# Shifted places for the halves of each weight piece, and wide and narrow matmuls in turn in every second FFN piece

## The chip, the cores and the metric

The kernel runs on one core of one Trainium2 chip. What counts is the device time of one execution, in microseconds (us). TensorE is called PE here (its weight loads PEld), VectorE is DVE, ScalarE is ACT, GpSimd is POOL and SyncE is SP.

## What is computed

Two blocks run one after the other on 256 rows of width 1024 in float32. Each has two layers, and each layer is an FFN, a mixer (attention and scan branches with gates) and a second FFN. Cut to the part that the change touches, one FFN is:

```
def swiglu(h, w_gate, w_up, w_down):
    a = h @ w_gate            # 256x1024 @ 1024x2816
    u = h @ w_up
    return (silu(a) * u) @ w_down      # 256x2816 @ 2816x1024

for l in range(2):                     # first block; the second has the same shape with layer norms
    x = x + 0.5 * swiglu(rms_norm(x), ...)
    x = x + hybrid_mixer(rms_norm(x), ...)     # input projection, three branches, gates, output projection
    x = x + 0.5 * swiglu(rms_norm(x), ...)
```

There are eight such FFNs in all. Every weight is used once, so some 500 MB of weights stream through the core.

## The kernel before, in words

**Precision in three products.** Weights and activations are float32. The kernel splits each into a high half of type float32r and a low half, the rest. A product is three matmuls: high activation with high weight, low activation with high weight, high activation with low weight.

**Pieces.** `plan()` cuts all weights into 938 pieces, numbered i, most of them 128 partitions by 1024 columns. SP loads blocks of up to two pieces into one of three `raw` buffers. ACT copies a piece into its high half (`whi`, L1777), and DVE, for a few pieces POOL, subtracts to get the low half (`wlo`, L2038 and L2498). There are five buffers of each half (`NHL = 5`), and piece i uses buffer i % 5 of both. Its halves are overwritten by those of piece i + 5, once PE has signalled the end of piece i (`mm`).

**Where buffers lie.** `LINE = 256`: the transposed activations (`xT_both`, `hT1`, `hT2`, `cq` and others) start at the same place within 256 bytes as the buffers `whi` and `wlo`. In the kernel before, raw, whi, wlo, xT_both and hT all start 128 bytes past a multiple of 256, and each of a piece's halves starts at the first byte of its buffer.

**PE's three ways to use a piece.** `rows` (L1544) loads a 128x128 block of the activations as the stationary operand and streams up to 512 columns of the weight piece. `columns` (L1563) loads 128 columns of the weight piece and streams 256 columns of activations. `wide` (L1579, L1585) does the FFN's gate and up projections: with 128 columns of `whi` loaded, one matmul streams 512 columns, the high and the low half of the activations together (called wide below); with 128 columns of `wlo` loaded, one streams 256, the high half alone (called narrow below). A piece holds four k-tiles of 256 columns, so `wide` issues eight wide matmuls into two PSUM banks and then eight narrow ones into the second halves of the same banks. Each of the eight FFNs has 20 chunks of two such pieces (320 pieces, 2560 wide and 2560 narrow matmuls); its first chunk and its down-projection use `rows`.

**What sets the order.** `Order` records one list of steps in program order, and each engine runs its own kinds of step from it. Halves are made up to four pieces ahead of the piece that PE works on. Every engine waits on semaphores; within `wide` PE waits for the high half at the start of a piece and for the low half ahead of the narrow matmuls.

Of the kernel before, what the change touches and what calls it, by code (L numbers as in the profile page):

```python
# [10 lines left out]
F32R = mybir.dt.float32r  # L11
# [8 lines left out]
PIECE = 1024  # L20
# [149 lines left out]
class Signals:  # L170
# [14 lines left out]
    def at(self, kind, *key):  # L185
        return self.sems[kind], self.value[(kind, key)] if self.sure else 0
# [54 lines left out]
        self.xt, self.H, self.L, self.nk, self.outs, self.free = xt, xt.H, xt.L, nk, outs, free  # L241


def memory(nc, ctx):

    m = {}

    def sbuf(name, shape, dt=F32, scope=ctx):
        m[name] = scope.enter_context(nc.sbuf_tensor(name, shape, dt))
        return m[name]  # L250

    def lined(name, scope=ctx):

        rest = (at_line - nc.sbuf_base) % LINE // 32 * 32
        if rest:
            scope.enter_context(nc.sbuf_tensor(name + "_rest", [128, rest // 4], F32))

    def halves(name, nk, scope=ctx):
        lined(name, scope)
        m[name] = Halves(name, sbuf(name + "_hi", [128, nk, 256], F32R, scope),  # L260
                         sbuf(name + "_lo", [128, nk, 256], F32R, scope), nk)

    def many(name, n, shape, dt=F32, scope=ctx):
        m[name] = [sbuf(f"{name}{i}", shape, dt, scope) for i in range(n)]

    m["ps"] = [ctx.enter_context(nc.psum_tensor(f"ps{i}", [128, 512], F32)) for i in range(8)]
    many("raw", NRAW, [128, BLOCK])
    many("whi", NHL, [128, PIECE], F32R)
    at_line = nc.sbuf_base % LINE
    many("wlo", NHL, [128, PIECE], F32R)  # L270
    many("x", 2, [128, D])
    sbuf("xn", [128, 2, D])
    sbuf("ident", [128, 128])
    sbuf("cols", [128, NCOLS])
    sbuf("stat", [128, 512])
    sbuf("phalf", [128, 2])
    lined("xT")
    both = sbuf("xT_both", [128, 2, 8, 256], F32R)
    m["xT"] = Halves("xT", both[:, 0, :, :], both[:, 1, :, :], 8, both)

    def ffn(block):
        with ExitStack() as ph:
            halves("hT" + block, 22, ph)
            many("h" + block, 3, [128, 2, 256], F32, ph)
            sbuf("row" + block, [128, 256], F32, ph)

    with ExitStack() as b1:
        sbuf("rope1", [128, 2, 64], F32, b1)
        sbuf("causal", [128, 384], F32, b1)
        sbuf("dist", [128, 4, 384], F32, b1)  # L290
        ffn("1")
        with ExitStack() as ph:
            sbuf("qk1", [128, 18, 256], F32, ph)
            sbuf("v1", [128, 2, 1152], F32, ph)
            sbuf("o_dil3", [128, 2, 768], F32, ph)
            sbuf("o_dil", [128, 2, 256], F32, ph)
            halves("oTa", 3, ph)
            halves("oTb", 3, ph)
            many("sm1_", 2, [128, 384], F32, ph)
            many("pr1_", 3, [128, 384], F32, ph)  # L300
            many("pt1_", 2, [128, 384], F32, ph)
            with ExitStack() as pm:
                sbuf("lat", [128, 2, 416], F32, pm)
                sbuf("q_mla", [128, 2, 576], F32, pm)
                sbuf("k_mla", [128, 2, 576], F32, pm)
                sbuf("v_mla", [128, 2, 384], F32, pm)
                halves("cq", 2, pm)
                halves("ckv", 1, pm)
                sbuf("rope_a", [128, 2, 96], F32, pm)
                sbuf("rope_b", [128, 2, 96], F32, pm)  # L310
                many("qkT", 2, [96, 512], F32, pm)
            sbuf("g1", [128, 2, 3072], F32, ph)
    many("vr", 2, [128, D])
    sbuf("strict", [128, 384])
    sbuf("chunk", [128, 384])
    sbuf("rope2", [128, 2, 32])
    sbuf("ends", [128, 384])
    ffn("2")
    with ExitStack() as ph:
        sbuf("oa", [128, 2, 1024], F32, ph)  # L320
        sbuf("ob", [128, 2, 1024], F32, ph)
        many("sm2_", 2, [128, 385], F32, ph)
        many("pr2_", 3, [128, 384], F32, ph)
        many("pt2_", 2, [128, 384], F32, ph)
        sbuf("rw", [128, 272], F32, ph)
        sbuf("g2", [128, 6144], F32, ph)
        with ExitStack() as reg2:
            sbuf("bc", [128, 4, 256], F32, reg2)
            sbuf("xd", [128, 2, 1024], F32, reg2)
            many("sums", 2, [128, 4, 256], F32, reg2)  # L330
            many("decay", 2, [128, 4, 384], F32, reg2)
            sbuf("cb", [128, 2, 384], F32, reg2)
            many("conv", 3, [128, 256], F32, reg2)
            many("rot", 2, [128, 512], F32, reg2)
            many("rot_t", 2, [128, 128], F32, reg2)
            sbuf("dt8", [128, 8, 16], F32, reg2)
        sbuf("qkc", [128, 16, 256], F32, ph)
        sbuf("vc", [128, 2, 1024], F32, ph)
        halves("oT2", 8, ph)
    return m  # L340


class Order:
# [53 lines left out]
    def halve(self, part):  # L397
        i = self.split[part]
        b, off, n = self.where[i]
        raw = self.m["raw"][b % NRAW][:, off:off + n]  # L400
        hi, lo = self.m["whi"][i % NHL][:, 0:n], self.m["wlo"][i % NHL][:, 0:n]
        if part == 0:
            self.do("hi", i, b, hi, raw)
        else:
            self.lo_of[i] = ("lo_p" if i in self.on_pool else "lo", i)
            self.do(self.lo_of[i][0], i, lo, raw, hi, self.hold)
        self.split[part] += 1
        self.ahead()
# [1118 lines left out]
def tensor_program(engine, sg, m, steps, *_):  # L1527
# [2 lines left out]

    def rows(i, t, job, lo_there, ready, banks):
        _, w, kts = pieces[i]
        hi, lo = m["whi"][i % NHL], m["wlo"][i % NHL]
        pe.wait_ge(*at("hi", i))
        for f in job.free[t]:
            pe.wait_ge(*at(*f))
        sl = slice(128 * t, 128 * t + 128)
        for n, (xs, ws) in enumerate(((job.H, hi), (job.L, hi), (job.H, lo))):
            if n == 2:
                pe.wait_ge(*at(*lo_there))  # L1540
            for j, (_, kt, _) in enumerate(kts):
                pe.wait_ge(*at(*ready[j]))
                for bank, c0, c1 in [job.outs[t][b] for b in banks if b < len(job.outs[t])]:
                    made = e.matmul(bank[:, 0:c1 - c0], xs[:, kt, sl], ws[:, j * w + c0:j * w + c1],  # L1544
                                    start=kt == 0 and n == 0, stop=kt == job.nk - 1 and n == 2)
        made.then_inc(*mark("mm", i, t, *(banks if banks == (0,) else ())))

    def columns(i, job, lo_there, ready):
        _, w, kts = pieces[i]
        hi, lo = m["whi"][i % NHL], m["wlo"][i % NHL]  # L1550
        pe.wait_ge(*at("hi", i))
        for freed in job.free:
            for f in freed:
                pe.wait_ge(*at(*f))
        for n, (ws, xs) in enumerate(((hi, job.H), (hi, job.L), (lo, job.H))):
            if n == 2:
                pe.wait_ge(*at(*lo_there))
            for j, (_, kt, _) in enumerate(kts):
                for there in ready[j]:
                    pe.wait_ge(*at(*there))  # L1560
                for c, out in enumerate(job.outs):
                    o = j * w + 128 * c
                    made = e.matmul(out, ws[:, o:o + 128], xs[:, kt, :], start=kt == 0 and n == 0 and c % 2 == 0,  # L1563
                                    stop=kt == job.nk - 1 and n == 2, skip_group_check=True)
        made.then_inc(*mark("mm", i, 1))

    def wide(i, job, lo_there, ready):
        _, w, kts = pieces[i]
        hi, lo = m["whi"][i % NHL], m["wlo"][i % NHL]
        pe.wait_ge(*at("hi", i))  # L1570
        for freed in job.free:
            for f in freed:
                pe.wait_ge(*at(*f))
        for j, (_, kt, _) in enumerate(kts):
            for there in ready[j]:
                pe.wait_ge(*at(*there))
            for c, bank in enumerate(job.outs):
                o = j * w + 128 * c
                e.matmul(bank[:, :].rearrange("p (n x) -> p n x", n=2), hi[:, o:o + 128], job.xt.both[:, :, kt, :],  # L1579
                         start=kt == 0, stop=False, skip_group_check=True)  # L1580
        pe.wait_ge(*at(*lo_there))
        for j, (_, kt, _) in enumerate(kts):
            for c, bank in enumerate(job.outs):
                o = j * w + 128 * c
                made = e.matmul(bank[:, 256:512], lo[:, o:o + 128], job.H[:, kt, :], start=False,  # L1585
                                stop=kt == job.nk - 1, skip_group_check=True)
        made.then_inc(*mark("mm", i, 1))

    def dt_rows(i, job, lo_there, ready):
        _, w, kts = pieces[i]  # L1590
        hi, lo = m["whi"][i % NHL], m["wlo"][i % NHL]
        pe.wait_ge(*at("hi", i))
        pe.wait_ge(*at(*lo_there))
        for f in job.free[0]:
# [1030 lines left out]
```

## Time and profile before

| what | value |
|---|---|
| device time, median of 2 runs | 2814.43 us (2814.07 to 2814.79) |
| span of the profiled execution | 2812.3 us |
| PE busy | 2792.6 us, 99% of the span, 15556 matmuls |
| PEld busy | 2396.6 us, 85% |
| DVE busy | 1921.3 us, 68% |
| ACT busy | 1554.0 us, 55% |
| POOL busy | 241.5 us, 9% |
| DMA | 503.82 MB, 50.2% of 16 engines' time on the weight queue |
| mean granted clock of PE | 0.999 |

The table tells what share of the span an engine was at work. The profile of one execution has its own time in its span alone, from the first to the last instruction; the device time of the runs lies 2.1 us above it. PE's matmuls overlap each other, so a busy share says little of how fast they follow one another: that is read from the starts in the timeline.

### The profile page before, as it was taken

Reading aid. Unit: us, or ns where it says so; the run is one execution under the profiler, and the core shown is the slowest. Engines: PE = TensorE matmul, PEld = TensorE weight load, DVE = VectorE, ACT = ScalarE, POOL = GpSimd, SP = SyncE. Lnnn points to the kernel's source line nnn. Section 1 sums busy time; section 2 is a strip of 40 time slices with the busy share of each in tenths; the row PEclk is TensorE's granted clock in tenths of the full one; section 3 lists DMA queues with packets and bytes.
Section 4 is the critical chain, followed back from the end, with each engine's and each line's share of the span. In section 5 each row is a group of like instructions: output and inputs, shape, how many; then the busy total and the mean of one; then the engine's idle time right before and its main releaser. Section 6 shows DMA issues by size and latency. Waiting matters only on the chain.

```text
span 2812.3 us, 40293 instructions
## 1 busy us (share of the span) xinstructions
PE 2792.6 (99%) x15556; PEld 2396.6 (85%) x15556; DVE 1921.3 (68%) x3180; ACT 1554.0 (55%) x2718; POOL 241.5 (9%) x187
## 2 busy tenths in 40 slices
PE   9999999999999999999999999999999999999998
PEld 8889888888889888888888987888888888878887
DVE  6756676747655667756568777776566687777765
ACT  6545656545545656545456556455455465655553
POOL 0010011010010011010014100110100141001100
PEclk9999999999999999999999999999999999999999
DMA  6544445555544345555554344555555554445553
GB/s 242 191 171 158 149 156 182 193 185 190 195 167 152 139 172 194 199 190 195 195 193 179 136 163 159 210 194 182 199 189 195 183 187 153 158 156 184 209 185 135
DMA packets 75055, 503.82 MB, mean 179 GB/s; under 512 B 8784, under 2 KB 10480, under 8 KB 19184
## 3 DMA queue, kind: packets, MB, share of 16 engines
q1 hardware_dynamic: 74576, 501.07, 50.2%
q8 instruction: 124, 2.03, 0.3%
q14 instruction: 67, 0.55, 0.1%
q10 hardware_dynamic: 288, 0.17, 0.0%
HBM read 500.12 MB, written 1.08 MB: 178 GB/s over the span
## 4 chain that ended last, share of the span: by engine, by line
PE 93%; DVE 4%; POOL 2%; issue 1%; ACT 1%; DMA 0%; SPq 0%; DVEq 0%; ACTq 0%
PE ps L1544 45%; PE ps L1579 21%; PE ps L1585 11%; PE ps L1563 9%; PE ps L1606 3%; POOL wlo L2498 2%; DVE wlo L2038 1%; PE ps L1701 1%; PE ps L1699 1%; DVE conv L2327 1%; PE ps L1726 1%; PE ps L1716 0%; PE ps L1717 0%; PE ps L1718 0%; DVE ps L2144 0%
## 5 line engine op out<-in xcount | busy, mean ns | idle before, releaser
L1777 ACT ACTIVATE whi<-raw 128x1024 fp32r<-128x1024 f32 (+3 forms) x938 | 977.5, 1045 | 600.3 <-PE ps L1544 426.1
L2038 DVE TENSOR_TENSOR wlo<-raw,whi 128x1024 fp32r<-128x1024 f32 (+2 forms) x894 | 1084.1, 1220 | 219.9 <-ACT whi L1777 218.9
L1579 PE MATMUL ps<-xT_both,whi 128*128 128x512 f32 x2560 | 641.6, 393 | 0.0
L1544 PE MATMUL ps<-whi,xT_both 128*128 128x512 f32 (+2 forms) x2336 | 628.9, 391 | 2.6 <-DVE xT_both L2061 1.6
L1579 PEld LDWEIGHTS ps<-xT_both,whi 128*128 128x128 f32 x2560 | 461.1, 189 | 82.6
L1544 PEld LDWEIGHTS ps<-whi,xT_both 128*128 128x128 f32 x2336 | 425.5, 188 | 83.7 <-issue 9.3
L1585 PEld LDWEIGHTS ps<-xT_both,wlo 128*128 128x128 f32 x2560 | 349.3, 191 | 24.9
L1585 PE MATMUL ps<-xT_both,wlo 128*128 128x256 f32 x2560 | 357.1, 282 | 0.0
L1544 PE MATMUL ps<-wlo,xT_both 128*128 128x512 f32 (+2 forms) x1168 | 354.6, 385 | 0.3 <-DVE wlo L2038 0.3
L2118 DVE TENSOR_TENSOR h<-h,ps 128x256 f32<-128x256 f32 x320 | 127.0, 418 | 203.1 <-ACT h L1826 203.1
L1544 PEld LDWEIGHTS ps<-wlo,xT_both 128*128 128x128 f32 x1168 | 218.4, 188 | 43.7 <-DVE wlo L2038 1.4
L1826 ACT ACTIVATE h<-ps 128x256 f32<-128x256 f32 x320 | 105.4, 382 | 214.1 <-PE ps L1585 214.1
L1544 PE MATMUL ps<-whi,hT_hi 128*128 128x512 f32 x704 | 221.5, 390 | 0.0
L1544 PE MATMUL ps<-whi,hT_lo 128*128 128x512 f32 x704 | 220.9, 389 | 0.0
L1544 PE MATMUL ps<-wlo,hT_hi 128*128 128x512 f32 x704 | 220.8, 389 | 0.0
L2498 POOL TENSOR_TENSOR wlo<-raw,whi 128x1024 fp32r<-128x1024 f32 (+1 forms) x44 | 102.5, 2347 | 1293.7 <-ACT whi L1777 1291.7
L1563 PE MATMUL ps<-xT_both,whi 128*128 128x256 f32 x1472 | 196.1, 286 | 1.0 <-DVE v_mla L2254 1.0
L1563 PEld LDWEIGHTS ps<-xT_both,whi 128*128 128x128 f32 x1472 | 182.9, 191 | 7.7 <-issue 6.9
L1544 PEld LDWEIGHTS ps<-wlo,hT_hi 128*128 128x128 f32 x704 | 132.2, 188 | 27.5
L1544 PEld LDWEIGHTS ps<-whi,hT_lo 128*128 128x128 f32 x704 | 132.2, 188 | 27.3
L1544 PEld LDWEIGHTS ps<-whi,hT_hi 128*128 128x128 f32 x704 | 131.7, 188 | 26.5
L1563 PE MATMUL ps<-xT_both,wlo 128*128 128x256 f32 x736 | 103.2, 283 | 0.0
(315 smaller groups left out, 2526.7 us busy)
## 6 DMA issues: line engine op xcount, KB each, us to landing
raw<-in_w SPq DMA_DIRECT2D x435, 1024.0 KB, 4.8
vr<-in_vrows SPq DMA_DIRECT2D x19, 512.0 KB, 5.6
raw<-in_w SPq DMA_DIRECT2D x12, 768.0 KB, 4.3
raw<-in_w SPq DMA_DIRECT2D x10, 896.0 KB, 4.5
sums<-scratch SPq DMA_DIRECT2D x8, 512.0 KB, 4.4
raw<-in_w SPq DMA_DIRECT2D x4, 832.0 KB, 4.4
raw<-in_w SPq DMA_DIRECT2D x4, 576.0 KB, 3.7
raw<-in_w SPq DMA_DIRECT2D x4, 512.0 KB, 6.9
```

Of the source, the lines that this page charges most:

```text
L1544: made = e.matmul(bank[:, 0:c1 - c0], xs[:, kt, sl], ws[:, j * w + c0:j * w + c1], start=kt == 0 and n == 0, stop=kt == job.nk - 1 and n == 2)
L1563: made = e.matmul(out, ws[:, o:o + 128], xs[:, kt, :], start=kt == 0 and n == 0 and c % 2 == 0, stop=kt == job.nk - 1 and n == 2, skip_gro ...
L1579: e.matmul(bank[:, :].rearrange("p (n x) -> p n x", n=2), hi[:, o:o + 128], job.xt.both[:, :, kt, :], start=kt == 0, stop=False, skip_grou ...
L1585: made = e.matmul(bank[:, 256:512], lo[:, o:o + 128], job.H[:, kt, :], start=False, stop=kt == job.nk - 1, skip_group_check=True)
L1606: return e.transpose(out, in_, ident[0:k, 0:k])
L1699: e.matmul(ps[:, 0:128], qT[:, 0:128], kT[:, 0:128], start=True, stop=True)
L1701: e.matmul(ps[:, 128:384], qT[:, 128:256], kT[:, 0:256], start=True, stop=True).then_inc(*mark("att", "s", *key))
L1777: e.activation(out, raw, ACT.Copy).then_inc(*mark("hi", i))
L1826: e.activation(h[:, n, :], banks[n][:, 256:512], ACT.Copy).then_inc(*mark("copy_a", "part", s, c, n))
L2038: e.tensor_tensor(out, raw, hi.bitcast(F32), sub).then_inc(*mark("lo", i))
L2118: e.tensor_tensor(h[:, n, :], h[:, n, :], banks[n][:, 0:256], add).then_inc(*mark("summed", s, c, n))
L2498: e.tensor_tensor(out, raw, hi.bitcast(F32), ALU.subtract).then_inc(*mark("lo_p", i))
```

## The change

Two things are changed. First, the halves of piece i no longer start at the first byte of their buffers: `upper` and `lower` add an offset of 0 to 240 bytes in steps of 16, another for each half and piece, and the buffers are 256 bytes longer for it. The place of everything else within 256 bytes stays as it was (all still start at 128). To make room, the scratch area for dynamic DMAs at the start of SBUF is set to 8192 bytes per partition, from 16384. Second, in `wide`, pieces with an odd number issue each narrow matmul right behind the wide one of the same k-tile and bank, and wait for both halves at the start of the piece. Even pieces stay as they were.

```diff
+SLACK = 64
+
+
+def upper(m, i):
+    at = 4 * ((7 * i + i // 16) % 16)
+    return m["whi"][i % NHL][:, at:at + PIECE]
+
+
+def lower(m, i):
+    at = 4 * ((3 * i + 5 * (i // 32)) % 16)
+    return m["wlo"][i % NHL][:, at:at + PIECE]
...
-    many("whi", NHL, [128, PIECE], F32R)
+    many("whi", NHL, [128, PIECE + SLACK], F32R)
     at_line = nc.sbuf_base % LINE
-    many("wlo", NHL, [128, PIECE], F32R)
+    many("wlo", NHL, [128, PIECE + SLACK], F32R)
...
-        hi, lo = self.m["whi"][i % NHL][:, 0:n], self.m["wlo"][i % NHL][:, 0:n]
+        hi, lo = upper(self.m, i)[:, 0:n], lower(self.m, i)[:, 0:n]
...
     def wide(i, job, lo_there, ready):
         _, w, kts = pieces[i]
-        hi, lo = m["whi"][i % NHL], m["wlo"][i % NHL]
+        hi, lo = upper(m, i), lower(m, i)
         pe.wait_ge(*at("hi", i))
         for freed in job.free:
             for f in freed:
                 pe.wait_ge(*at(*f))
+        woven = i % 2 == 1
+        if woven:
+            pe.wait_ge(*at(*lo_there))
         for j, (_, kt, _) in enumerate(kts):
             for there in ready[j]:
                 pe.wait_ge(*at(*there))
...
                 e.matmul(bank[:, :].rearrange("p (n x) -> p n x", n=2), hi[:, o:o + 128], job.xt.both[:, :, kt, :],
                          start=kt == 0, stop=False, skip_group_check=True)
-        pe.wait_ge(*at(*lo_there))
-        for j, (_, kt, _) in enumerate(kts):
-            for c, bank in enumerate(job.outs):
-                o = j * w + 128 * c
-                made = e.matmul(bank[:, 256:512], lo[:, o:o + 128], job.H[:, kt, :], start=False,
-                                stop=kt == job.nk - 1, skip_group_check=True)
+                if woven:
+                    made = e.matmul(bank[:, 256:512], lo[:, o:o + 128], job.H[:, kt, :], start=False,
+                                    stop=kt == job.nk - 1, skip_group_check=True)
+        if not woven:
+            pe.wait_ge(*at(*lo_there))
+            for j, (_, kt, _) in enumerate(kts):
+                for c, bank in enumerate(job.outs):
+                    o = j * w + 128 * c
+                    made = e.matmul(bank[:, 256:512], lo[:, o:o + 128], job.H[:, kt, :], start=False,
+                                    stop=kt == job.nk - 1, skip_group_check=True)
         made.then_inc(*mark("mm", i, 1))
...
-    nc = _bacc.Bacc("TRN2", target_bir_lowering=False, num_devices=1)
+    nc = _bacc.Bacc("TRN2", target_bir_lowering=False, num_devices=1, dynamic_dma_scratch_size=8192)
```

`rows`, `columns` and `dt_rows` take `hi, lo = upper(m, i), lower(m, i)` in the same way.

This is PE's order in the first FFN before, behind the first chunk of two pieces: two pieces (an even and an odd one), each with its wide matmuls (L1579) and then its narrow ones (L1585).

```order
L1579 MATMUL ps<-xT_both,whi 128x512 [waits s_hi]
L1579 MATMUL ps<-xT_both,whi 128x512 x7
L1585 MATMUL ps<-xT_both,wlo 128x256 [waits s_lo]
L1585 MATMUL ps<-xT_both,wlo 128x256 x7
L1579 MATMUL ps<-xT_both,whi 128x512 [waits s_hi]
L1579 MATMUL ps<-xT_both,whi 128x512 x7
L1585 MATMUL ps<-xT_both,wlo 128x256 [waits s_lo]
L1585 MATMUL ps<-xT_both,wlo 128x256 x7
```

The same two pieces now (wide matmuls are L1595, narrow ones L1605 in an even piece and L1598 in an odd one); the odd piece's last pairs are left out.

```order
L1595 MATMUL ps<-xT_both,whi 128x512 [waits s_hi]
L1595 MATMUL ps<-xT_both,whi 128x512 x7
L1605 MATMUL ps<-xT_both,wlo 128x256 [waits s_lo]
L1605 MATMUL ps<-xT_both,wlo 128x256 x7
L1595 MATMUL ps<-xT_both,whi 128x512 [waits s_lo,s_hi]
L1598 MATMUL ps<-xT_both,wlo 128x256
L1595 MATMUL ps<-xT_both,whi 128x512
L1598 MATMUL ps<-xT_both,wlo 128x256
L1595 MATMUL ps<-xT_both,whi 128x512
L1598 MATMUL ps<-xT_both,wlo 128x256
```

In the odd piece the wait for the low half moved from behind eight wide matmuls to the start of the piece, and the narrow matmuls moved up between the wide ones. The end of the first FFN's last chunk, where PE goes on to the down-projection, now reads:

```order
L1595 MATMUL ps<-xT_both,whi 128x512
L1598 MATMUL ps<-xT_both,wlo 128x256
L1595 MATMUL ps<-xT_both,whi 128x512
L1598 MATMUL ps<-xT_both,wlo 128x256
L1557 MATMUL ps<-whi,hT_hi 128x512 [waits s_summed,s_xlo,s_hi]
```

A narrow matmul is still the last of the chunk, so what waits for the chunk's end waits for the same instruction. The other engines issue the same instructions in the same order.

## Rows read from the trace of the kernel before

**Rows 1.** the page: span, busy share of each engine, granted clock in slices.

```profile
span 2812.3 us, 40293 instructions
...
PE 2792.6 (99%) x15556; PEld 2396.6 (85%) x15556; DVE 1921.3 (68%) x3180; ACT 1554.0 (55%) x2718; POOL 241.5 (9%) x187
...
PEclk9999999999999999999999999999999999999999
```

**Rows 2.** the page's chain that ended last, shares of the span by line.

```profile
PE ps L1544 45%; PE ps L1579 21%; PE ps L1585 11%; PE ps L1563 9%; PE ps L1606 3%; POOL wlo L2498 2%; DVE wlo L2038 1%; PE ps L1701 1%; PE ps L1699 1%; DVE conv L2327 1%; PE ps L1726 1%; PE ps L1716 0%; PE ps L1717 0%; PE ps L1718 0%; DVE ps L2144 0%
```

**Rows 3.** groups by line and shape: count | busy us, mean ns | idle before.

```profile
L1579 PE MATMUL ps<-xT_both,whi 128*128 128x512 f32 x2560 | 641.6, 393 | 0.0
L1544 PE MATMUL ps<-whi,xT_both 128*128 128x512 f32 x2080 | 571.7, 397 | 1.0 <-ACT whi L1777 0.8
...
L1585 PE MATMUL ps<-xT_both,wlo 128*128 128x256 f32 x2560 | 357.1, 282 | 0.0
...
L1544 PE MATMUL ps<-wlo,xT_both 128*128 128x512 f32 x1040 | 321.5, 390 | 0.3 <-DVE wlo L2038 0.3
L1544 PE MATMUL ps<-whi,hT_hi 128*128 128x512 f32 x704 | 221.5, 390 | 0.0
...
L1563 PE MATMUL ps<-xT_both,whi 128*128 128x256 f32 x1472 | 196.1, 286 | 1.0 <-DVE v_mla L2254 1.0
```

**Rows 4.** timeline of PE in FFN pieces: start us, length us, operation, count.

```profile
64.19 2.00 PE L1579 MATMUL ps<-xT_both,whi 128*128 128x512 f32 x8
66.03 1.12 PE L1585 MATMUL ps<-xT_both,wlo 128*128 128x256 f32 x8
66.99 2.00 PE L1579 MATMUL ps<-xT_both,whi 128*128 128x512 f32 x8
...
69.78 2.00 PE L1579 MATMUL ps<-xT_both,whi 128*128 128x512 f32 x8
```

**Rows 5.** timeline of PE, the last two wide matmuls of one piece.

```profile
65.58 0.61 PE L1579 MATMUL ps<-xT_both,whi 128*128 128x512 f32 x2
```

**Rows 6.** timeline of PE in the down-projection, 512 columns throughout.

```profile
141.76 0.61 PE L1544 MATMUL ps<-wlo,hT_hi 128*128 128x512 f32 x2
...
144.48 0.61 PE L1544 MATMUL ps<-wlo,hT_hi 128*128 128x512 f32 x2
```

**Rows 7.** timeline of PE at the pieces of 256 columns, L1563.

```profile
1469.85 2.08 PE L1563 MATMUL ps<-xT_both,whi 128*128 128x256 f32 x16
...
1481.37 0.59 PE L1737 MATMUL ps<-bc 128*128 128x256 f32 x2
1481.80 0.39 PE L1738 MATMUL ps<-bc 128*128 128x128 f32 x2
```

**Rows 8.** timeline of PE at the piece with 16-column weight loads.

```profile
1451.88 0.39 PE L1600 MATMUL ps<-xT_both,whi 128*16 128x256 f32 x2
...
1454.69 2.07 PE L1563 MATMUL ps<-xT_both,whi 128*128 128x256 f32 x16
```

**Rows 9.** timeline of PE at the pieces of 288 columns.

```profile
218.13 0.43 PE L1544 MATMUL ps<-whi,cq_hi 128*128 128x288 f32 x2
...
221.06 0.43 PE L1544 MATMUL ps<-wlo,cq_hi 128*128 128x288 f32 x2
```

**Rows 10.** groups of DVE by line and shape.

```profile
L2038 DVE TENSOR_TENSOR wlo<-raw,whi 128x1024 fp32r<-128x1024 f32 x852 | 1051.8, 1240 | 218.7 <-ACT whi L1777 217.7
...
L2122 DVE TENSOR_TENSOR h<-h,row 128x256 f32<-128x256 f32 x80 | 34.1, 426 | 2.7
...
L2438 DVE TENSOR_TENSOR pr<-pr,sm 128x384 f32<-128x384 f32 x32 | 17.9, 559 | 1.1
```

**Rows 11.** timeline of ACT over the same FFN pieces.

```profile
69.98 1.07 ACT L1777 ACTIVATE whi<-raw 128x1024 fp32r<-128x1024 f32 x1 [0.88 <-PE ps L1585]
```

**Rows 12.** timeline of DVE over the same pieces, two of its halvings.

```profile
64.62 1.22 DVE L2038 TENSOR_TENSOR wlo<-raw,whi 128x1024 fp32r<-128x1024 f32 x1
...
70.20 1.22 DVE L2038 TENSOR_TENSOR wlo<-raw,whi 128x1024 fp32r<-128x1024 f32 x1
```

More of the change, by code:

```diff
@@ L1549, in columns @@
         _, w, kts = pieces[i]
-        hi, lo = m["whi"][i % NHL], m["wlo"][i % NHL]
+        hi, lo = upper(m, i), lower(m, i)
         pe.wait_ge(*at("hi", i))
@@ L1568, in wide @@
         _, w, kts = pieces[i]
-        hi, lo = m["whi"][i % NHL], m["wlo"][i % NHL]
+        hi, lo = upper(m, i), lower(m, i)
         pe.wait_ge(*at("hi", i))
@@ L1590, in dt_rows @@
         _, w, kts = pieces[i]
-        hi, lo = m["whi"][i % NHL], m["wlo"][i % NHL]
+        hi, lo = upper(m, i), lower(m, i)
         pe.wait_ge(*at("hi", i))
```

## The prediction, made before the changed kernel ran

> **What bounds the kernel now.** I read the page first: PE is busy for 2792.6 of 2812.3 us at full granted clock in every slice [rows 1], and the chain that ended last runs through PE's piece lines, L1544, L1579, L1585 and L1563, for 86% of the span [rows 2]. Then the groups by line: the matmuls that use weight pieces waited about 1 us for anything, those of the FFN nothing at all [rows 3]. So the time is the number of matmuls by the distance from one start to the next, and only a change of that distance moves it. A busy mean (393 ns for a wide matmul) is not that distance, since matmuls overlap. I take it from starts in the timeline:
>
> - 512 columns in the down-projection: from 141.76 to 144.48 us lie 12 matmuls, 226.7 ns each [rows 6]. 512 columns at 2.4 GHz are 213.3 ns, so each carries 13.3 ns more.
> - 256 columns: from 1469.85 to 1481.37 us four pieces of 24, 96 matmuls, 120.0 ns each [rows 7]. Columns are 106.7, and again 13.3 more.
> - An even and an odd FFN piece: 64.19 to 69.78 us is 5.59, so 2.795 us a piece [rows 4]. At 226.7 and 120.0 its sixteen matmuls would take 8 x 346.7 = 2.773 us. The odd 20 ns are in the wide ones: the first six take 64.19 to 65.58, 231.7 ns each, the last two 0.45 us, 225 to 227 each [rows 4, 5]. After the step from narrow to wide PE needs some matmuls to come to its steady distance. The narrow ones take (66.99 - 66.03) / 8 = 120.
>
> **The change part by part.**
>
> *Alternation.* It adds and removes no matmul: 160 of the 320 pieces, so 1280 pairs, are issued in another order. A pair costs 2.795 / 8 = 349.4 ns now. If each matmul keeps its steady distance whatever stands ahead of it, a pair costs 346.7 and the change brings 1280 x 2.7 ns = 3.5 us. The trace before has no wide matmul behind a single narrow one. Lower end: that, and the even pieces too lose their slow first six (30 ns x 160 = 4.8 us) because they no longer follow eight narrow ones: -8.3 us. Upper end: every wide matmul in a pair pays the 231.7 of a first one, 351.7 a pair: +2.9 us. I take -4 us, near the steady sum, since the step from wide to narrow shows nothing of the kind, and give the even pieces little, because an odd piece's end is still a narrow matmul.
>
> The narrow matmul now adds into the same 256 PSUM columns as the wide one just ahead. A row bears on that: the piece of 16-column loads puts three matmuls of 256 columns in a row into the same columns, and its 24 take 1451.88 to 1454.69, 117.1 ns each [rows 8], no more than 120. So no term for it. Nor does a shorter time between weight loads bind: eight narrow ones in a row already load 128 columns every 120 ns.
>
> The wait for the low half comes 1.84 us earlier in odd pieces. The cover: the piece ends at 69.78; ACT takes its buffer at 69.98 [rows 11]; DVE makes low halves in pairs 5.58 us apart (64.62 and 70.20, [rows 12]), so the one for the freed buffer stands at the latest near 74.3 (a third one, 4.1 us behind 70.20, as the first of the next pair) and ends by 75.5. PE comes to that piece four pieces later, at 69.78 + 4 x 2.795 = 80.96. Some 5 us are left where 1.84 are lost: no stall, 0 us. If that cover were gone, a woven piece would stand for up to 1.2 us (one halving); the place to see it is the first chunk of an FFN. The end of an odd piece is its last narrow matmul as before, so ACT and the buffers behind it are released at the same point; the raw buffers, and with them SP's loads, depend on ACT and DVE, whose order is unchanged.
>
> *Places.* Every one of the matmuls on pieces reads one operand (the stationary one in the FFN and in `columns`, the streamed one in `rows`) at another place within 256 bytes than now, nearly always another than that of its partner. The rows of [rows 3] are 2560 + 2560 of the FFN, 2080 + 1040 + 3 x 704 of `rows` (the 704 appear for each of the three products) and 1472 plus half as many with the low half: 12,560 matmuls; with the smaller groups some 13,300, of which some 8,200 have 512 columns. The trace has places other than 128 for three of such operands. In the pieces of 288 columns the second k-tile starts 1152 bytes on, so at 0 instead of 128; 22 matmuls take 218.13 to 221.06, 133.2 ns each, which is 120 of columns and the same 13.2 [rows 9]. The 16-column loads move by 64 bytes each and keep 117 [rows 8]. On DVE, L2438 reads an operand 4 bytes off: 559 ns for 384 columns, where 256 at an even place take 426 and 1024 take 1240 [rows 10], by which line 384 would be 562. None shows a cost, but no row has PE at a multiple of 16 that is not one of 64. I take 0, from the nearest rows. Upper bound: PE stays at the distance of its slow starts wherever it has 512 columns: 5.0 ns x 8,200 = +41 us. Lower bound: all go at the 117.1 of [rows 8] against 120: -2.9 ns x 13,300 = -39 us.
>
> The Trainium skill, "SBUF — State Buffer", section on who interferes with whom, gives PE two independent read ports, one for the streamed operand and one for the weight load. By it the relative place of the two can't matter, and the sum stays where the rows put it.
>
> ACT and DVE write the shifted halves. DVE sits idle for 218.7 us ahead of its halving, waiting for ACT [rows 10], so a few ns more on 938 of them stay covered. The smaller DMA scratch only moves addresses.
>
> *Sum.* The profiled execution's span is 2812.3 us; -4 + 0 gives 2808.3. The device time's median, 2814.43, lies 2.1 above the span; adding that gives **2810 us**.
>
> **Rivals.**
>
> *A, slower: shifted weights keep PE off its steady distance.* Mechanism: PE's steady distance depends on both operands of a matmul lying alike within 256 bytes, as all of them do now; at another place each matmul of 512 columns pays the 5 ns of a slow start. For it: those 5 ns exist and are of that size whatever buffer is read [rows 4, 5]. Against: the two places of [rows 9]. Time: 2810 + 41 = 2851. It decides from 0.3 ns a matmul on, where it eats the 4 us. A heavier form, in which a shifted weight load doubles the 13.3 ns, gives 13,300 x 13.3 = +177 us, 2987; past 2% it needs 4.5 ns on all. Chance 0.17 for the first, 0.06 for forms past 2%.
>
> *B, faster: the 13.3 ns are a collision that the new places dissolve.* For it: a float32 matmul of 256 columns (L1737) takes (1481.80 - 1481.37) / 2 = 215 ns, twice 106.7 and only 1.6 more, with weight loads of the same 128 columns [rows 7]; so the 13.3 are not due to every matmul. Against: 256, 288 and 512 columns carry the same 13.3, which looks like a fixed step and not like a collision that depends on where two streams meet. In full it gives 11.7 ns x 13,300 = -156 us, 2654; in part (117.1 for 120) 2810 - 39 = 2771. Chance 0.10 for the part, 0.05 for more than 2%. The Trainium skill, "TensorE: Matmul & The Clock Gate", section on the back-to-back issue gap, gives N/2.4 + 2.5 ns, which is 215.8 for 512 columns; this trace disagrees by 10.9 ns, and by that rule this rival is the one that restores the gap.
>
> *C, alternation costs: every wide one pays for the narrow one ahead of it.* 2814.4 + 2.9 = 2817, with places at nothing. Chance 0.12, a part of the 0.62 below.
>
> *D, the change does nothing:* 2814. It shares the forecast's range.
>
> **How the numbers follow.** Forecast with places at nothing (D and C with it): 0.62, between 2803 and 2820, likeliest 2810. A to 2851: 0.17, A past 2%: 0.06. B in part: 0.10, B past 2%: 0.05. About 2%, 56 us, is what a measurement of this kernel can tell from no change. Faster by over that: 0.05; slower: 0.06; within: 0.89. The range takes in the partial forms of A and B, **2775 to 2851**, and leaves out the far forms and a slice of the partial ones.
>
> **What would show it.** Odd pieces: the distance between the starts of two narrow matmuls in a woven piece near 346.7 ns; even pieces at 2.77 to 2.80 us; no idle ahead of L1595 and L1598. Down-projection still 226.7 ns and `columns` 120.0, whatever i is. DVE's halving still near 1240 ns, ACT's near 1.07 us. It would be wrong if distances differed from piece to piece with a period of 16, or if the down-projection, which alternation does not touch, moved.

## The result, and the profile after

The changed kernel takes 2836.83 us (median of 2 runs, 2836.57 to 2837.09) where the kernel before takes 2814.43: 1.008 times as long, 95% interval [1.0051, 1.0109]. It is slower by 22 us. The forecast was 2810 us, faster by 4.

The page of the changed kernel, its span, busy engines and chain by line, to be held against [rows 1, 2]:

```profile
span 2835.3 us, 40453 instructions
...
PE 2816.9 (99%) x15556; PEld 2390.6 (84%) x15556; DVE 1921.7 (68%) x3180; ACT 1554.7 (55%) x2718; POOL 239.3 (8%) x187
...
PE ps L1557 46%; PE ps L1595 21%; PE ps L1576 8%; PE ps L1605 5%; PE ps L1598 5%; PE ps L1626 3%; POOL wlo L2518 2%; DVE conv L2347 1%; DVE wlo L2058 1%; PE ps L1721 1%; PE ps L1719 1%; PE ps L1746 1%; ACT whi L1797 0%; ACT conv L1969 0%; PE ps L1736 0%
```

PE is still at work 99% of the span, and the chain still runs through the piece lines (L1557 is L1544 of before, L1576 is L1563, L1595 is L1579, L1605 and L1598 are L1585). The span is 23.0 us longer, PE's busy time 24.3, with the same 15556 matmuls. PE doesn't wait more: its groups by line (count, then busy us and mean ns, then idle us before) have the same idle time as in [rows 3]. DVE's halving costs what it did in [rows 10], and waits 12 us longer in all for ACT, off PE's path.

```profile
L2058 DVE TENSOR_TENSOR wlo<-raw,whi 128x1024 fp32r<-128x1024 f32 x852 | 1051.3, 1239 | 230.3 <-ACT whi L1797 229.0
...
L1595 PE MATMUL ps<-xT_both,whi 128*128 128x512 f32 x2560 | 771.2, 394 | 0.0
L1557 PE MATMUL ps<-whi,xT_both 128*128 128x512 f32 x2080 | 578.8, 400 | 1.1 <-ACT whi L1797 0.9
...
L1557 PE MATMUL ps<-whi,hT_hi 128*128 128x512 f32 x704 | 224.9, 395 | 0.0
```

So the distances have grown. The down-projection, which alternation doesn't touch, in the timeline of PE (start us, length us, operation, count):

```profile
141.83 0.62 PE L1557 MATMUL ps<-whi,hT_hi 128*128 128x512 f32 x2
...
144.61 0.62 PE L1557 MATMUL ps<-whi,hT_hi 128*128 128x512 f32 x2
```

Twelve matmuls take 2.78 us here, 231.7 ns each, where [rows 6] have 226.7. Its single distances were 226 or 227 ns in 95 of 100 cases before, and are so in 6 of 100 now: nearly all lie anywhere from 224 to 241. An FFN stretch, to be held against [rows 4]: an odd piece, an even one and the start of the next.

```profile
64.88 0.39 PE L1595 MATMUL ps<-xT_both,whi 128*128 128x512 f32 x1
65.11 0.28 PE L1598 MATMUL ps<-xT_both,wlo 128*128 128x256 f32 x1
65.23 0.39 PE L1595 MATMUL ps<-xT_both,whi 128*128 128x512 f32 x1
...
67.66 2.01 PE L1595 MATMUL ps<-xT_both,whi 128*128 128x512 f32 x8
69.51 1.11 PE L1605 MATMUL ps<-xT_both,wlo 128*128 128x256 f32 x8
70.46 0.40 PE L1595 MATMUL ps<-xT_both,whi 128*128 128x512 f32 x1
```

The woven piece takes 64.88 to 67.66, 2.78 us, the even one 67.66 to 70.46, 2.80. Neither is far from the 2.795 of before. Summed over all matmuls on pieces, from each start to the next start on PE:

| matmuls | before, us (mean ns) | changed, us (mean ns) | difference, us |
|---|---|---|---|
| down-projection, 512 columns, x2110 | 479.3 (227.1) | 490.5 (232.5) | +11.2 |
| other row pieces, 512 columns, x3648 | 855.7 (234.6) | 869.0 (238.2) | +13.3 |
| FFN, wide, x2560 | 589.5 (230.3) | 594.4 (232.2) | +4.9 |
| FFN, narrow, x2560 | 304.8 (119.1) | 301.4 (117.7) | -3.4 |
| columns, 256 columns, x2208 | 270.2 (122.4) | 267.2 (121.0) | -3.0 |
| row pieces of 288, x48 | 6.7 (139.2) | 6.7 (139.2) | 0 |

The first column has the group, its columns per matmul and how many distances were summed. The whole loss stands in the pieces that PE streams (`rows`), at 512 columns. Where PE loads the piece and streams activations, the sum is -1.5 us.

### The profile page after: what moved, and what is told of

The parts are those of the page before. It is cut to its first block, busy times and chain, and to the rows that moved or that the text cites. A ratio compares the mean times of both kernels' runs of the same rounds, so it can differ in the third digit from the quotient of the medians.

```text
span 2835.3 us, 40453 instructions
## 1 busy us (share of the span) xinstructions
PE 2816.9 (99%) x15556; PEld 2390.6 (84%) x15556; DVE 1921.7 (68%) x3180; ACT 1554.7 (55%) x2718; POOL 239.3 (8%) x187
## 4 chain that ended last, share of the span: by engine, by line
PE 93%; DVE 4%; POOL 2%; ACT 1%; issue 0%; DMA 0%; SPq 0%; DVEq 0%; ACTq 0%
PE ps L1557 46%; PE ps L1595 21%; PE ps L1576 8%; PE ps L1605 5%; PE ps L1598 5%; PE ps L1626 3%; POOL wlo L2518 2%; DVE conv L2347 1%; DVE wlo L2058 1%; PE ps L1721 1%; PE ps L1719 1%; PE ps L1746 1%; ACT whi L1797 0%; ACT conv L1969 0%; PE ps L1736 0%
## 5 line engine op out<-in xcount | busy, mean ns | idle before, releaser
L2058 DVE TENSOR_TENSOR wlo<-raw,whi 128x1024 fp32r<-128x1024 f32 (+2 forms) x894 | 1083.7, 1219 | 231.5 <-ACT whi L1797 230.3
L1595 PE MATMUL ps<-xT_both,whi 128*128 128x512 f32 x2560 | 771.2, 394 | 0.0
L1557 PE MATMUL ps<-whi,xT_both 128*128 128x512 f32 (+2 forms) x2336 | 636.3, 394 | 2.7 <-DVE xT_both L2081 1.6
L1595 PEld LDWEIGHTS ps<-xT_both,whi 128*128 128x128 f32 x2560 | 470.1, 188 | 98.3
L1557 PEld LDWEIGHTS ps<-whi,xT_both 128*128 128x128 f32 x2336 | 425.8, 188 | 90.4 <-issue 9.3
L1557 PE MATMUL ps<-wlo,xT_both 128*128 128x512 f32 (+2 forms) x1168 | 359.0, 388 | 0.3 <-DVE wlo L2058 0.3
L1598 PE MATMUL ps<-xT_both,wlo 128*128 128x256 f32 x1280 | 358.1, 280 | 0.0
L1557 PEld LDWEIGHTS ps<-wlo,xT_both 128*128 128x128 f32 x1168 | 218.7, 188 | 47.3 <-DVE wlo L2058 1.2
L1598 PEld LDWEIGHTS ps<-xT_both,wlo 128*128 128x128 f32 x1280 | 240.9, 188 | 0.1
L1557 PE MATMUL ps<-whi,hT_hi 128*128 128x512 f32 x704 | 224.9, 395 | 0.0
L1557 PE MATMUL ps<-whi,hT_lo 128*128 128x512 f32 x704 | 224.6, 395 | 0.0
L1557 PE MATMUL ps<-wlo,hT_hi 128*128 128x512 f32 x704 | 224.2, 394 | 0.0
L1576 PE MATMUL ps<-xT_both,whi 128*128 128x256 f32 x1472 | 194.4, 284 | 1.0 <-DVE v_mla L2274 1.0
L1576 PEld LDWEIGHTS ps<-xT_both,whi 128*128 128x128 f32 x1472 | 181.2, 189 | 7.8 <-issue 6.9
L1605 PEld LDWEIGHTS ps<-xT_both,wlo 128*128 128x128 f32 x1280 | 173.5, 188 | 14.0
L1605 PE MATMUL ps<-xT_both,wlo 128*128 128x256 f32 x1280 | 177.1, 280 | 0.0
L1557 PEld LDWEIGHTS ps<-wlo,hT_hi 128*128 128x128 f32 x704 | 132.3, 188 | 31.4
L1557 PEld LDWEIGHTS ps<-whi,hT_lo 128*128 128x128 f32 x704 | 132.3, 188 | 30.8
```

The costliest lines, as they stand in the source:

```text
L2058: e.tensor_tensor(out, raw, hi.bitcast(F32), sub).then_inc(*mark("lo", i))
```

## The experiments

All run on the chip beside the kernel before. "Places" are the offsets of a piece's halves in their buffers. Every one keeps the longer buffers and the small DMA scratch, so only the places and the alternation differ. FFN pieces are given by their mean length from the starts of all 320.

**One part alone.** Theory 1: the places cost the time. Theory 2: alternation does. Places only:

```diff
-        woven = i % 2 == 1
+        woven = False
```

> Even and odd FFN pieces both as before (all wide, then all narrow), places of the halves as in the changed kernel. Theory 1 (the places cost it): the changed kernel's trace has 232.5 ns between matmuls of 512 columns in the down-projection where before has 227.1, and 238.2 for 234.6 in the other row pieces; both stay, and the time is 2836 to 2841 us. Theory 2 (alternation costs it, in the FFN or by what it leaves behind): 2812 to 2816 us and 227 ns in the down-projection.

Measured: 2838.56 us, ratio 1.0086 [1.0071, 1.0101]. Down-projection 232.5 ns, other row pieces 238.2, FFN pieces 2804 ns. The places alone make 24.2 us, more than the whole loss. Theory 2 falls as the main cause. Alternation only:

```diff
-    at = 4 * ((7 * i + i // 16) % 16)
+    at = 0
...
-    at = 4 * ((3 * i + 5 * (i // 32)) % 16)
+    at = 0
```

> All halves start at the first byte of their (longer) buffers, the small DMA scratch stays, odd FFN pieces alternate. Theory 1 (places): the down-projection is back at 226.7 ns and the time is 2809 to 2813 us, since a pair in steady distance takes 346.7 ns instead of 349.4. Theory 2 (alternation): 2830 us or more. Theory 3 (neither, but the moved addresses or the smaller scratch): also above 2830, with 232 ns in the down-projection.

Measured: 2817.99 us, 1.0013 [1.0003, 1.0022]: slower by 3.7 us, not faster by 3.5. The down-projection is back at 227.1 ns. The timeline of PE from a woven piece to the next:

```profile
64.89 0.40 PE L1595 MATMUL ps<-xT_both,whi 128*128 128x512 f32 x1
65.13 0.28 PE L1598 MATMUL ps<-xT_both,wlo 128*128 128x256 f32 x1
65.24 0.40 PE L1595 MATMUL ps<-xT_both,whi 128*128 128x512 f32 x1
65.48 0.28 PE L1598 MATMUL ps<-xT_both,wlo 128*128 128x256 f32 x1
65.61 0.40 PE L1595 MATMUL ps<-xT_both,whi 128*128 128x512 f32 x1
...
67.72 1.98 PE L1595 MATMUL ps<-xT_both,whi 128*128 128x512 f32 x8
69.55 1.12 PE L1605 MATMUL ps<-xT_both,wlo 128*128 128x256 f32 x8
70.50 0.40 PE L1595 MATMUL ps<-xT_both,whi 128*128 128x512 f32 x1
```

The woven piece takes 64.89 to 67.72, 2.83 us or 354 ns a pair. The narrow matmul starts some 240 ns behind the wide one (64.89 to 65.13, 65.24 to 65.48), 236.7 on the mean of all woven pieces, where the steady sum had 226.7; the next wide one starts 117.4 behind the narrow one, for 120. The even piece behind it takes 67.72 to 70.50, 2.78 us, so its wide matmuls do lose their slow start: (69.55 - 67.72) / 8 is 229. Over all pieces odd ones take 2832 ns and even ones 2780, where before all took 2795. That is +22 ns for two pieces, +3.6 us for 160 such pairs of pieces.

**What is left when both are gone.**

```diff
-        woven = i % 2 == 1
+        woven = False
...
+    at = 0
...
+    at = 0
```

> All halves at the first byte of their longer buffers, no alternation, the small DMA scratch: what is left of the change are moved addresses. Theory 1: the times of before, 2813 to 2815.5 us, with FFN pieces at 2795 ns. Theory 3 (the addresses or the scratch cost something): 2817 us or more, which would take over what the run with alternation alone showed.

Measured: 2813.97 us, 0.9999 [0.999, 1.0008], FFN pieces 2795 ns, down-projection 227.1. The longer buffers, moved addresses and smaller scratch cost nothing.

**All pieces alternate.**

```diff
-        woven = i % 2 == 1
+        woven = True
```

(with both places at 0)

> All halves at the first byte, and all 320 FFN pieces alternate instead of every second. With every second, woven pieces took 2832 ns and the unwoven ones between them 2775, where all took 2794 before: +20 ns for each two pieces, +3.2 us. Theory 1 (alternation itself costs 38 ns a piece and the unwoven ones gain only by following it): all at 2832 ns, 320 x 38 = +12 us, 2825 to 2828 us. Theory 2 (the cost lies in changing between the two orders): 2814 or less.

Measured: 2825.24 us, 1.0038 [1.0025, 1.0051], FFN pieces 2829 ns. Eight pairs of that run:

```profile
64.29 0.40 PE L1595 MATMUL ps<-xT_both,whi 128*128 128x512 f32 x1
64.52 0.28 PE L1598 MATMUL ps<-xT_both,wlo 128*128 128x256 f32 x1
64.64 0.40 PE L1595 MATMUL ps<-xT_both,whi 128*128 128x512 f32 x1
...
67.11 0.40 PE L1595 MATMUL ps<-xT_both,whi 128*128 128x512 f32 x1
```

From 64.29 to 67.11 they take 2.82 us, 352.5 ns a pair. Nothing changes between orders here, so alternation itself costs some 34 ns a piece. What in it costs is not separated. A narrow matmul in a woven piece follows a wider one and also adds into the PSUM columns that the wide one just ahead wrote; the cost sits in the distance between these two, and every run that alternates does both.

**Which operand.** The changed kernel's places for streamed pieces only, then for loaded (stationary) pieces only. `LOADED` holds the numbers of the pieces used by `wide`, `columns` and `dt_rows`.

```diff
+LOADED = {i for i, (key, w, _) in enumerate(plan()) if key[0] in ("qk1", "xbc", "qc", "kc") or w == 256 or key[0] == "dt"}
...
-    at = 4 * ((7 * i + i // 16) % 16)
+    at = 0 if i in LOADED else 4 * ((7 * i + i // 16) % 16)
...
```

The same is done in `lower`, and alternation is off, here and in all runs below.

> No alternation. Pieces that PE streams (row pieces and the down-projection) have the changed kernel's places, pieces that PE loads as stationary (the FFN's gate and up, and columns) start at the first byte. Theory 1 (a streamed operand away from the loaded one's place costs, a loaded one does not): the down-projection's 2110 matmuls at 232.5 ns for 227.1 give +11 us and the 3648 other ones at 238.2 for 234.6 +13, so 2837 to 2840 us. Theory 2 (the loaded operand's place costs the larger part): 2820 or less.

Measured: 2838.27 us, 1.0085 [1.0071, 1.0099]. Down-projection 232.5 ns, other row pieces 238.1, FFN pieces as before. The opposite half:

```diff
...
+    at = 4 * ((7 * i + i // 16) % 16) if i in LOADED else 0
...
```

> The opposite half: stationary pieces have the changed kernel's places, streamed ones start at the first byte; no alternation. Theory 1: the down-projection is back at 227.1 ns; FFN pieces cost 2804 ns for 2795 (+3 us), columns give back 3 us: 2812 to 2816 us. Theory 2: 2825 or more.

Measured: 2814.02 us, 1.0 [0.9991, 1.0009]. FFN pieces 2804 ns, +3 us, and columns 121.0 ns, -3 us. The down-projection in the two runs, streamed only first:

```profile
141.87 0.63 PE L1560 MATMUL ps<-whi,hT_hi 128*128 128x512 f32 x2
...
144.66 0.63 PE L1560 MATMUL ps<-whi,hT_hi 128*128 128x512 f32 x2
```

```profile
141.78 0.61 PE L1560 MATMUL ps<-whi,hT_lo 128*128 128x512 f32 x2
...
144.50 0.61 PE L1560 MATMUL ps<-whi,hT_lo 128*128 128x512 f32 x2
```

Twelve matmuls take 2.79 us (232.5 ns each) in the one and 2.72 (226.7) in the other. The whole +24 us comes with the streamed pieces.

**Variety or distance, and in what steps.** One place for all:

```diff
+    at = 4
...
+    at = 4
```

> No alternation; both halves of every piece start 16 bytes into their buffers, one place for all, but another than that of the activations. Theory 1a (what counts is that a matmul's two operands lie alike): every matmul of 512 columns keeps about 5 ns, down-projection 232 ns, 2836 to 2840 us. Theory 1b (what counts is that the place changes from piece to piece): 226.7 ns and 2813 to 2816 us.

Measured: 2834.62 us, 1.0073 [1.0058, 1.0088]. The down-projection is at 231.9 ns: that the place changes from piece to piece is not what costs. The time lies 1.4 us below the range expected; FFN pieces are at 2793 ns, three of the eight FFNs at 2760 a piece. Four steps of 64 bytes:

```diff
+    at = 16 * ((7 * i + i // 16) % 4)
...
+    at = 16 * ((3 * i + 5 * (i // 32)) % 4)
```

> No alternation; places change from piece to piece by the same formulas, but in four steps of 64 bytes instead of sixteen of 16. Theory 1c (only the place within 64 bytes counts): down-projection at 226.7 ns, 2813 to 2816 us. Theory 1d (the place within 256 bytes counts): about 232 ns and 2834 to 2840 us.

Measured: 2829.78 us, 1.0055 [1.004, 1.007], down-projection 231.9 ns. To lie alike within 64 bytes is not enough. It is 9 us faster than with steps of 16, and 4 below the range expected; 3.3 of them are in FFN pieces (2793 ns) and 2.6 in columns (119.8 ns).

This trace also tells one place from another. By the formulas, the first sixteen pieces of the third FFN's down-projection have both halves at the same offset, 0, 192, 128 and 64 bytes by turns. Here are the starts of four pieces and of the fifth, and the middle of the first:

```profile
753.08 0.63 PE L1557 MATMUL ps<-whi,hT_hi 128*128 128x512 f32 x2
...
754.47 0.62 PE L1557 MATMUL ps<-whi,hT_hi 128*128 128x512 f32 x2
...
755.83 0.63 PE L1557 MATMUL ps<-whi,hT_hi 128*128 128x512 f32 x2
...
758.63 0.62 PE L1557 MATMUL ps<-whi,hT_hi 128*128 128x512 f32 x2
...
761.42 0.62 PE L1557 MATMUL ps<-whi,hT_hi 128*128 128x512 f32 x2
...
764.17 0.63 PE L1557 MATMUL ps<-whi,hT_hi 128*128 128x512 f32 x2
```

Pieces at 192 take 2.80 us (755.83 to 758.63, 233.3 ns a matmul), at 128 bytes 2.79 (232.5), at 64 bytes 2.75 (229.2). A piece at 0, where both operands lie alike, takes 2.75 too, but it starts slow and is at 226.7 in its second half (754.47 to 755.83, six matmuls). All sixteen pieces follow this pattern. So 128 bytes apart is not alike; the cost is not one figure but depends on the distance in bytes; and a piece that lies alike among pieces that don't needs some five matmuls of its twelve to come back, so varied places cost in its time too.

**To the partner, or in itself.** All halves 32 bytes on (`at = 8`), first with the activations moved along, then without:

```diff
-    at_line = nc.sbuf_base % LINE
+    at_line = (nc.sbuf_base + 32) % LINE
```

> No alternation. Every half starts 32 bytes into its buffer, and the activations (xT, hT and the other pairs of halves) are moved by 32 bytes too, so both operands of each matmul again lie alike within 256 bytes, at 160 instead of 128. Theory 1a (the distance depends on how the streamed operand lies to the loaded one): down-projection 227.1 ns, 2812 to 2816 us. Theory 1e (the streamed operand's own place within 256 bytes counts): about 232 ns and 2830 to 2838 us.

> The control to it: halves 32 bytes into their buffers, activations where they were; no alternation. Both theories: down-projection about 232 ns, 2828 to 2838 us. If it stays at 227, half a line of 64 bytes is harmless and the run with activations moved says nothing.

Measured: 2814.60 us, 1.0001 [0.9992, 1.001], with them; 2847.42 us, 1.0117 [1.0103, 1.013], without, 9 us above the range expected of the control. The down-projection in each, moved together first:

```profile
141.84 0.62 PE L1557 MATMUL ps<-whi,hT_lo 128*128 128x512 f32 x2
...
144.56 0.62 PE L1557 MATMUL ps<-whi,hT_lo 128*128 128x512 f32 x2
```

```profile
141.71 0.63 PE L1557 MATMUL ps<-whi,hT_lo 128*128 128x512 f32 x2
...
144.51 0.63 PE L1557 MATMUL ps<-whi,hT_lo 128*128 128x512 f32 x2
```

2.72 us for twelve against 2.80, 226.7 against 233.3 ns. With both operands at 128 or both at 160 the distance is the same, with one at each it is longer: it depends on how a matmul's streamed operand lies to the loaded one, not on where either lies, as far as these two places tell. That being alike within 256 bytes is enough shows in the run with 2813.97 us: its buffers are 4352 bytes long, so neighbours lie 256 bytes apart within 512, and the down-projection is at 227.1 ns all the same. FFN pieces take 2815 ns in the run without (+6.5 us), where the loaded operand is the one that lies 32 bytes on.

**Places used on purpose.** Streamed pieces at 0, loaded ones all 16 or all 64 bytes on:

```diff
+    at = 4 if i in LOADED else 0      # the first run
...
+    at = 16 if i in LOADED else 0     # the second
```

> Stationary pieces all start 16 bytes into their buffers, streamed ones at the first byte; no alternation. With all halves at 16, three of the eight FFNs ran at 2760 ns a piece (wide matmuls at 227 from the first on) and five at 2810 by turns. Theory 1 (the streamed place alone costs, the loaded place only moves PE between patterns that hold themselves up): down-projection 227.1 ns; with all eight FFNs in the fast pattern 2800 to 2804 us, with three of eight 2810 to 2813. Theory 2 (any difference between the operands costs): 2820 or more.

Measured: 2812.89 us (2810.4 to 2815.15), 0.9995 [0.9986, 1.0004], no difference on the median. Two FFNs ran at 2760 ns a piece, six at 2804 and 2816 by turns; the mean is 2798. The same code in the first FFN and in the fifth:

```profile
64.14 1.98 PE L1598 MATMUL ps<-xT_both,whi 128*128 128x512 f32 x8
...
66.90 1.98 PE L1598 MATMUL ps<-xT_both,whi 128*128 128x512 f32 x8
```

```profile
1321.16 2.02 PE L1598 MATMUL ps<-xT_both,whi 128*128 128x512 f32 x8
...
1323.96 2.03 PE L1598 MATMUL ps<-xT_both,whi 128*128 128x512 f32 x8
```

2.76 us a piece against 2.80 here. The third piece, where PE comes from other work (transposes), takes 2856 ns in the two fast FFNs and 2902 in the others, and the pattern behind it stays to the FFN's end; what chooses it was not tested.

> As the run with stationary pieces at 16 bytes and streamed ones at the first byte, but stationary pieces at 64. In the runs with varied places narrow matmuls whose weights lie 64 bytes further than the stream took 116 ns for 120. Theory 1 (loaded places only choose among patterns): 2807 to 2813 us with FFN pieces below 2794 ns on the mean; at 2774 to 2800 ns by turns as in the run with steps of 64 it would be 2811. Against it: FFN pieces at 2800 or more and a time above 2816.

Measured: 2798.95 us, 0.9945 [0.9933, 0.9958]: faster than both kernels, by 15.5 us than the one before. It is 8 us below the best case that I expected. Its timeline, FFN and columns:

```profile
64.18 2.02 PE L1598 MATMUL ps<-xT_both,whi 128*128 128x512 f32 x8
66.04 1.07 PE L1608 MATMUL ps<-xT_both,wlo 128*128 128x256 f32 x8
66.95 2.02 PE L1598 MATMUL ps<-xT_both,whi 128*128 128x512 f32 x8
68.81 1.07 PE L1608 MATMUL ps<-xT_both,wlo 128*128 128x256 f32 x8
69.72 2.02 PE L1598 MATMUL ps<-xT_both,whi 128*128 128x512 f32 x8
```

```profile
1466.77 1.07 PE L1579 MATMUL ps<-xT_both,wlo 128*128 128x256 f32 x8
...
1473.12 0.59 PE L1760 MATMUL ps<-bc 128*128 128x256 f32 x2
```

An FFN piece takes 64.18 to 69.72 halved, 2.77 us, in all eight FFNs. The wide matmuls are no faster (1.86 us for eight, 232.5 ns); the narrow ones take (66.95 - 66.04) / 8 = 114 ns where [rows 4] have 120. Columns take (1473.12 - 1466.77) / 56 = 113.4 where [rows 7] have 120.0. Summed over the trace: narrow -12.6 us, columns -10.5, wide +7.0, row pieces +1.0.

## Why the prediction was wrong

**What bounds it** held. Time is matmuls by distance; no wait grew, and PE's idle time is the same.

**The places, taken at 0 us,** is the step that failed. They cost +24 us (2838.6 against 2814.3), and the sign that I had named for being wrong came with them: the down-projection moved. Rival A had the mechanism right: a matmul of 512 columns is at its steady distance only if both operands lie alike within 256 bytes, and otherwise pays about 5 ns on the mean of the changed kernel's places (2 at 64 bytes apart, 6.6 at 32 and at 192). It was priced on all 8,200 of them and given 0.17. The runs give 5.4 ns on the 2110 of the down-projection and 3.6 on the 3648 other streamed ones, which had slow starts already; the FFN's 2560 wide ones, where the shifted operand is the loaded one, pay 2 ns, and narrow ones pay half of that back. (The prediction's counts, 13,300 matmuls on pieces and 8,200 of 512 columns, are 13,592 and 8,320 in the trace; it changes nothing.) So 2851 was too much and 2814 too little.

The error was in what I let stand for the missing row. The 288-column pieces of [rows 9] do stream from another place, and kept 133.2 ns; after the change, with places of every kind, they keep the mean they had (139.2). Their mean doesn't feel the place in any run here (139.0 to 139.4) and could say nothing of 512 columns. Nor could the 16-column loads of [rows 8], nor DVE's L2438. The row that did speak was [rows 4, 5]: 232 ns were possible in this kernel.

**The ports.** The Trainium skill, "SBUF — State Buffer", section on who interferes with whom, gives PE two independent read ports. That the relative place can't matter was my inference from it, and the runs contradict the inference: 226.7 ns when both operands lie at 160, 233.3 when the streamed one alone does. What in PE's path makes the difference was not measured, nor whether the ports have a part in it.

**Alternation, taken at -4 us,** was the smaller failure: alone it costs +3.7 us. Rival C, at 0.12, had the sign. A pair took 354 ns and not 346.7, beyond my upper end of 351.7: in strict alternation the narrow matmul starts 232 to 241 ns behind the wide one, never settling to 226.7. The term was too small from the start: I priced a first wide matmul at 231.7, the mean of six, where the trace before has 233 and 236 (medians) for the first and the second of a piece. The second half of the argument was right and too small: even pieces gained 15 ns each by following a woven one (30 had been the lower end). In the presence of shifted places, where nothing is steady, the sign turns: 2836.8 with alternation, 2838.6 without, and FFN pieces 2799 ns for 2804. The two terms do not add (24.2 and 3.7 against 22.4 together).

**Left open:** the 0 for adding into the same PSUM columns. The narrow matmul's own distance to the next wide one is no longer than before (117.4 ns), but such a cost would sit ahead of it, where the distance is 10 ns over the steady one; the three matmuls of [rows 8] speak against it, of 256 columns alone.

**What held:** the wait for the low half cost nothing, with no idle ahead of L1595 and L1598; ACT, DVE and the scratch cost nothing (2813.97). **Rival B** had a true core that I saw nowhere near its place: the 13.3 ns are not fixed. With the loaded operand 64 bytes on, 256 columns take 113.4 ns, 6.7 above the columns themselves, over half of the way from 13.3 to the 1.6 of the float32 matmul in [rows 7]. It needs one chosen place; the mean over sixteen gives 1.4 ns. (Those 215 ns are of one instruction and not of a whole float32 matmul: the kernel calls L1737 four times and the trace has eight records of it, so 256 columns in float32 take 430 ns. The 1.6 per instruction stands.)

## What to carry to other kernels

Where PE is the bound and streams float32r with a weight load for each matmul, the place of the two operands relative to each other within 256 bytes is a knob: here it moved the time from 0.5% faster (loaded pieces 64 bytes on) to 1.2% slower (all pieces 32 bytes on). In such a kernel, keep streamed weights of 512 columns alike with what is loaded, try constant shifts for the pieces that are loaded, and measure distances between starts, not busy means. A row bears on a price only if it is of the same size and the same operand; before using one as a bound, ask whether it would have moved. Two terms that both act on PE's steady distance must be measured together.

## What the hardware showed that was not expected

- The same twelve 512-column matmuls take 2.72 us with both operands at one place within 256 bytes (128 or 160) and 2.78 to 2.80 with the streamed one 16 or 32 bytes away. By bytes apart, one matmul takes 226.7 ns at 0, 229 at 64, 232.5 at 128 and 233.3 at 32 and at 192.
- After a piece at another place a stream that lies alike is back at 226.7 ns only after some five matmuls, as behind the narrow matmuls of [rows 4, 5].
- The loaded operand's place works the other way at 256 columns: 120.0 ns alike, 113.4 at 64 bytes apart; FFN pieces as a whole take 2795 ns alike, 2815 at 32, 2777 at 64 bytes.
- At 16 bytes the same instructions run in one of two patterns, 2760 or 2810 ns a piece, chosen where the FFN is entered and kept for 37 pieces. The runs of that kernel also scatter more (2810.4 to 2815.15 us) than those of any other here.
- Alike within 256 bytes is enough and within 64 or 128 is not. Why, and which part of PE's path it belongs to, is open.
